# Splitting the merged tiles earlier, a longer own tail in the output projection, and weight units split one step sooner in the recurrent layer

## The reference

```python
# first model, each layer
merged = (gates[:, :, 0] * (y_a @ w_pa[l])
          + gates[:, :, 1] * (y_b @ w_pb[l])
          + gates[:, :, 2] * (y_c @ w_pc[l]))
x = x + merged @ w_o[l]
h = rms_norm(x, g_ffn[l])
x = x + (jax.nn.silu(h @ w1[l]) * (h @ w3[l])) @ w2[l]

# second model, recurrent layer (6 blocks of 256 channels)
proj = x @ w_in
y_branch, u = jnp.split(proj, 2, axis=-1)
y_branch = jax.nn.gelu(y_branch, approximate=True)
u = conv4(u) + conv_b
r, i = sigmoid(gates(u))
log_a = -LRU_C * r * jax.nn.softplus(-a_param)
a = jnp.exp(log_a)
b = jnp.sqrt(-jnp.expm1(2.0 * log_a)) * (i * u)
h = scan(a, b)              # h[t] = a[t] * h[t-1] + b[t]
return (h * y_branch) @ w_out

# second model, behind each mixer and each network
x = x + rms_norm_2(m, norm_g[layer, 1])
```

## Time and profile before

| what | value |
|---|---|
| median of 3 runs | 3479.68 us (3471.39, 3479.68, 3499.27) |
| profiled execution | 3500.03 us, its span 3498.2 us |
| TensorE busy | 3414.9 us, 98% of the span |
| VectorE / ScalarE / GpSimd busy | 45% / 34% / 10% |
| mean granted TensorE clock | 0.982 of full speed |

### The profile page before, as it was taken

The page is one execution under the profiler, slowest core; times in us unless marked ns, Lnnn a source line. Parts: engine busy times, 40 slices in busy tenths (PEclk is TensorE's granted clock), DMA queues, the critical chain, the costliest instruction groups (busy, mean ns, idle before and its releaser), DMA issues.

```text
span 3498.2 us, 41531 instructions
## 1 busy us (share of the span) xinstructions
PE 3414.9 (98%) x17076; PEld 2817.6 (81%) x17076; DVE 1576.8 (45%) x2298; ACT 1186.5 (34%) x1931; POOL 339.0 (10%) x309
## 2 busy tenths in 40 slices
PE   8999999999999999999999999999999998999998
PEld 7777887788887867887888888888888887788887
DVE  5454444443445452444433443343533357764234
ACT  4334322322324242323322332222422236643222
POOL 2120000100020110000000110001200031130001
PEclk9999999999999997999999999999999999999999
DMA  4120222222231211222222222222232222222222
GB/s 150 61 73 30 69 98 91 90 97 97 92 104 61 81 40 35 73 97 85 92 98 99 93 98 76 88 82 73 79 102 97 97 73 73 91 85 94 93 97 78
DMA packets 83242, 295.47 MB, mean 84 GB/s; under 512 B 9616, under 2 KB 11888, under 8 KB 82928
## 3 DMA queue, kind: packets, MB, share of 16 engines
q1 hardware_dynamic: 80352, 283.85, 24.1%
q0 software_dynamic: 2704, 8.98, 0.8%
HBM read 289.61 MB, written 3.18 MB: 84 GB/s over the span
## 4 chain that ended last, share of the span: by engine, by line
PE 89%; DVE 5%; ACT 4%; issue 1%; POOL 1%; DMA 0%; SPq 0%; DVEq 0%; ACTq 0%; POOLq 0%
PE bank L2289 26%; PE bank L2291 25%; PE bank L2290 25%; PE bank L2534 3%; PE bank L2502 3%; PE bank L2511 2%; DVE w_lo L1745 1%; PE bank L2648 1%; ACT w_hi L1340 1%; DVE arena L2199 1%; PE bank L2442 1%; ACT arena L1519 1%; PE bank L2358 1%; PE bank L2636 0%; ACT arena L1378 0%
## 5 line engine op out<-in xcount | busy, mean ns | idle before, releaser
L1745 DVE TENSOR_TENSOR w_lo<-raw_ring,w_hi 128x1024 fp32r<-128x1024 f32 x530 | 674.7, 1274 | 1302.6 <-ACT w_hi L1340 1301.7
L2289 PE MATMUL bank<-h_hi,w_hi 128*128 128x512 f32 (+1 forms) x2752 | 1075.9, 391 | 42.9 <-DVE w_lo L1745 19.1
L2290 PE MATMUL bank<-h_lo,w_hi 128*128 128x512 f32 (+1 forms) x2752 | 1060.7, 385 | 0.0
L2291 PE MATMUL bank<-h_hi,w_lo 128*128 128x512 f32 (+1 forms) x2752 | 1060.4, 385 | 0.0
L1340 ACT ACTIVATE w_hi<-raw_ring 128x1024 fp32r<-128x1024 f32 x530 | 559.9, 1057 | 1154.2 <-PE bank L2291 1079.1
L2289 PEld LDWEIGHTS bank<-h_hi,w_hi 128*128 128x128 f32 x2752 | 524.2, 190 | 155.2 <-issue 32.4
L2290 PEld LDWEIGHTS bank<-h_lo,w_hi 128*128 128x128 f32 x2752 | 524.2, 190 | 102.5 <-issue 3.1
L2291 PEld LDWEIGHTS bank<-h_hi,w_lo 128*128 128x128 f32 x2752 | 523.5, 190 | 103.3
L2289 PE MATMUL bank<-act_hi,w_hi 128*128 128x512 f32 (+1 forms) x1336 | 508.7, 381 | 10.6 <-DVE act_lo L1758 7.6
L2291 PE MATMUL bank<-act_hi,w_lo 128*128 128x512 f32 (+1 forms) x1336 | 505.4, 378 | 0.0
L2290 PE MATMUL bank<-act_lo,w_hi 128*128 128x512 f32 (+1 forms) x1336 | 505.3, 378 | 0.0
(11 more groups left out here) (195 smaller groups left out, 2720.4 us busy)
## 6 DMA issues: line engine op xcount, KB each, us to landing
raw_ring<-weights SPq DMA_DIRECT2D x530, 512.0 KB, 3.3
arena<-rpb POOLq DMA_DIRECT2D x16, 320.0 KB, 4.3
xs<-x_t SPq DMA_DIRECT2D x8, 256.0 KB, 6.5
out_t<-xs SPq DMA_DIRECT2D x16, 128.0 KB, 1.8
arena<-block SPq DMA_DIRECT2D x1, 1024.0 KB, 9.6
arena<-o_nat POOLq DMA_DIRECT2D x2, 512.0 KB, 3.4
arena<-ret POOLq DMA_DIRECT2D x4, 256.0 KB, 3.1
o_nat<-arena POOLq DMA_DIRECT2D x2, 384.0 KB, 3.1
```

The lines of the kernel that those rows point to most:

```text
L1745: nc.vector.tensor_tensor(w_slot(w_lo, u), raw_slot(u), f32(w_slot(w_hi, u)), ALU.subtract) \
L2289: nc.tensor.matmul(out, lhs[0], rhs[0], start=first, stop=False)
L2290: nc.tensor.matmul(out, lhs[0], rhs[1], start=False, stop=False)
L2291: return nc.tensor.matmul(out, lhs[1], rhs[0], start=False, stop=last)
```

## The change

Four edits; no arithmetic is added or taken away.

1. `MERGED_EARLY = 6`: ScalarE and VectorE split merged tiles 0 to 5 between `("pr", 7, 1)` and the last gate, and only tiles 6 and 7 after `("pr", 7, 2)`.
2. `WO_TAIL = 4`: in the output projection the last four k tiles run group by group.
3. Recurrent layer: ScalarE splits one unit between the two high parts of the convolution and no longer between the two gelu; VectorE splits one more unit between the two scans of a block, and none between the two row products.
4. `post_norm`: the squares of X tiles 0 to 3 move behind the high parts of tiles 4 to 7, those of 4 to 7 behind everything; ScalarE splits a unit after the high part of tile 5, VectorE splits it between the low parts of tiles 6 and 7 and no longer ahead of both.

```diff
+WO_TAIL = 4
+MERGED_EARLY = 6
...
-    together = n - 2 if keys[0][1] == "wo" else n
+    together = n - WO_TAIL if keys[0][1] == "wo" else n
...
                     following_hi(1, k)
+                    if k == 5:
+                        upto(first[-1], 2, 1)
+                    if k >= NT:
+                        square(X[k - NT], tile(SQ2 + k - NT), D ** -0.5)
+                upto(first[-1], 5, 1)
+                for k in range(NT, KD):
                     square(X[k], tile(SQ2 + k), D ** -0.5)
-                    if k in (5, 7):
-                        upto(first[-1], 2 if k == 5 else 5, 1)
...
+                        if (m, b) == (KD - 1, 2):
+                            before((l, "pr", KD - 1, 1))
+                            wait_acc(act, (l, "pr", KD - 1, 1))
+                            merged_hi(l, range(MERGED_EARLY))
                         copy_out((l, "gate", m, b), tile(GATE + 3 * (m % 2) + b), func=ACT.Sigmoid)
...
                 before((l, "pr", KD - 1, 2))
                 wait_acc(act, (l, "pr", KD - 1, 2))
-                for m in range(KD):
-                    act.wait_ge(merged_ready, KD * l + m + 1)
-                    hi(("merged", l, m), part(act_hi, m), tile(MERGED + m))
+                merged_hi(l, range(MERGED_EARLY, KD))
...
-                    def conv_hi(n):
+                    def conv_hi(n, between=None):
                         for i in (2 * n, 2 * n + 1):
+                            if between and i % 2:
+                                before(between)
                             act.wait_ge(conv_ready, i + 1)
...
-                            conv_hi(n + 1)
+                            conv_hi(n + 1, ("ly", 2 * n + 3) if n else None)
...
-                    if j in (2 * KD - 1, 2 * KD + 1):
-                        upto(first[-1], 2 if j < 2 * KD else 5, 1)
+                    if j >= 2 * KD:
+                        upto(first[-1], 2 if j == 2 * KD else 5, 1)
...
                     if kind == "gate":
+                        if (m, i) == (KD - 1, 2):
+                            merged_lo(l, range(MERGED_EARLY))
                         rows_scaled((l, "gate", m, i))
...
-                            conv(n + 1, [("lg", n, 1, 0), ("ly", 2 * n + 2) if n else ("lu", 4)])
+                            conv(n + 1, [("ly", 2 * n + 2), ("ly", 2 * n + 3)] if n else [("lg", 0, 1, 0), ("lu", 4)])
...
                         for i in pair:
-                            before(after)
+                            before(("lg", n + 1, 0, 0) if i % 2 and n < LRU_BLOCKS - 2 else after)
```

More of the change, by code:

```diff
@@ L1561, in first_inputs, with merged_hi @@
                     square(X[k], tile(SQ1 + k), D ** -0.5)
+            def merged_hi(l, ms):
+                for m in ms:
+                    act.wait_ge(merged_ready, KD * l + m + 1)
+                    hi(("merged", l, m), part(act_hi, m), tile(MERGED + m))
             for l in range(DEPTH):
@@ L2043, in ffn, with merged_lo @@
                         lo_x(*following[:2], KD - 1, following[2])
+            def merged_lo(l, ms):
+                for m in ms:
+                    lo(("merged", l, m), part(act_lo, m), tile(MERGED + m), part(act_hi, m))
             dve.wait_ge(consts_in, 16)
@@ L2123, in _ @@
                         then(ins)
-                for m in range(KD):
-                    lo(("merged", l, m), part(act_lo, m), tile(MERGED + m), part(act_hi, m))
+                merged_lo(l, range(MERGED_EARLY, KD))
                 for m in range(KD):
```

## The result

| what | before | after |
|---|---|---|
| median | 3480.95 us (17 runs, 3466.68 to 3502.69) | 3450.96 us (17 runs, 3441.54 to 3473.41) |
| profiled execution | 3500.03 us | 3471.89 us, its span 3470.1 us |
| mean granted TensorE clock in it | 0.982 | 0.985 |

The ratio is 0.9906, its 95% interval 0.9881 to 0.993: 0.9% faster. The forecast was 3452.3 us, and 3472.6 us for a profiled execution with the long stretch at half clock.

What follows compares the result with a forecast made beforehand. TensorE, busy 98% of the span, bounds the kernel; only its waits and half-clock time can be won back. -21.4 (projections) - 6.9 (recurrent layer) + 0.9 (norms) = -27.4 us, from 3479.7 to 3452.3; range 3437 to 3475.

Steps and rivals of the forecast that it cites:

- the long stretch at half clock: First model, from the second attention group: 28.9 us lost in the profiled execution's layer 1; rival puts it in median, chance 0.28.
- the forecast case: Whole kernel: median 3452.3 us, own range 3444 to 3461, chance 0.45.
- No wait: End of the output projection: VectorE keeps up, so TensorE does not wait for the last tiles.
- The next product wants tile 7 only at its last k tile: Behind the output projection: tile 7 is wanted only 4.8 us into the next product.
- the sum of 3.4 us: Behind the projection's last group: unit 1.23, addition 0.68, high part 0.73, low part 0.75, plus handover.
- two signs of being right: Both projection stretches: 54 to 55 us for 240 matmuls, and no wait on the low parts of X.
- the 21.4 of the sum: Projection stretches of both layers: edits 1 and 2 win back all lost time, 9.4 and 12.0 us.
- The lap of 31.71: Recurrent layer: time from square roots to square roots before the change, forecast to become 30.0 us.
- The new waits ahead of lg: Recurrent layer: TensorE waits for lg(n+1)'s unit about 2.8 us a block, around 5 in the first.
- the ring opens: Rival, recurrent layer: it becomes TensorE's, 20.7 us won there, -41.2 in all, 3438.5 us; chance 0.09.
- the bound of -6: Second model's norms: uncontended operations take 0.48 + 1.23 + 0.48, both waits vanish, 2.0 us a norm won.
- Nothing in the edits speaks for or against: Rival that the half-clock stretch falls into the median run: edits give no reason either way, 3472.6 us; chance 0.28.

Runs made afterwards that it cites:

- z_after_wait: Changed kernel, with VectorE's four low parts made ahead of its two weight units in layer 1's attention: 3442.55 us.
- y_wait: Kernel before, with only VectorE's four low parts made ahead of its two weight units in layer 1's attention: median 3466.28 us.
- x_norm2: Changed kernel, with ScalarE's squares of tiles 0 to 3 behind all high parts in the three norms, so GpSimd adds later: 3436.8 us.
- e3_ring: Kernel before with the third edit alone, the recurrent layer: 3471.53 us, ratio 0.9998.
- e4_norms: Kernel before with the fourth edit alone, the three norms of the second model: 3476.76 us, ratio 0.9992.
- e1_merged: Kernel before with the first edit alone, six merged tiles split while the last gate's product runs: 3458.97 us, ratio 0.9944.
- e2_wo: Kernel before with the second edit alone, the output projection's last four k tiles group by group: 3457.59 us, ratio 0.9940.

## Why the prediction was right

**The time.** 3450.96 against 3452.3: right, and by the forecast case. A part of it is luck, since two errors cancel. The forecast started from 3479.7, the middle one of three runs; in the 17 runs of the comparison those without the long stretch have a median of 3472.9, and those of the changed kernel one of 3449.6, 23.3 less. Between z_after_wait and y_wait it is 23.7, not 27.4. The rest of the 30.0 us between the medians comes from the long stretch, which fell into fewer runs: 2 of 17 against 7 of 17 of before. The forecast left it where it was.

**Edit 1: right, step by step.** Six high parts took 3.24 us (forecast 3.2), six low parts 3.70 (3.7), the last gate was taken up at 584.20 (584.6), and no wait followed. Together with edit 2 the clock stayed at 1.00 in both stretches, as forecast.

**Edit 2: right in size, wrong in "No wait".** The step that failed is "The next product wants tile 7 only at its last k tile". It looked at tile 7 alone. In the program the low part of tile 6 stands behind the addition of tile 7, and that behind the unit; TensorE wants tile 6 one k tile sooner. Nor did the sum of 3.4 us hold VectorE's idle time for w_hi, 1.60, and the longer w_lo, 2.00 for 1.23. What remained was 0.96 us a layer, 1.40 with the handover (55.80 less 54.40), so two signs of being right did not come: 54 to 55 us, and no wait on the low parts of X. The other error went the other way: the stretch before takes 66.3 to 66.4 us in layer 0 too in three other executions of the same code, not 63.8. Together: 2 x (66.37 - 55.80) = 21.1, against the 21.4 of the sum: two errors of 2 to 3 us that cancel. In the two profiled executions it was 18.6 (8.0 and 10.6).

**Edit 3: right.** From the roots of block 0 to those of block 4 are 119.00 us, where before (2912.89 to 3038.68) there were 125.79: 6.79 less, forecast 6.9. (The lap of 31.71 that the forecast took is the longest of four from 31.03, and the new ones are 29.40, 29.62, 30.36 and 29.62, not 30.0; in the sum this cancels.) The new waits ahead of lg were forecast at 5 in the first block and 2.8 behind it; they are 5.13, 0.55 and 2.90. The 0.55 stands behind a piece at half clock of 3.4 us, in which TensorE's own work took 1.7 us longer: the wait was filled, and the lap stayed nearly the ring's (29.62, with 30.36 for the next). The rival "the ring opens" is refuted: even with the lap cut to 28.96 the wait stays.

**Edit 4: right.** Forecast +0.3 a norm, with a wait of some 2 us ahead of tile 7. The wait is 2.32. Between the same waits, in pairs of traces with as much half-clock time, the three stretches behind the norms are longer by 0.3 us each (379.8 against 379.5, 50.1 against 49.8, 370.1 against 369.8): +1.0 against +0.9. With GpSimd's additions moved behind them the three operations were in time (x_norm2), so the reason for rejecting the bound of -6 was right.

**The long stretch: right in size, wrong in "Nothing in the edits speaks for or against".** The profiled execution had it and took 3471.89 (forecast with it 3472.6); the median had not. The wait behind which it begins, 1.75 us, was in the trace already, and the prediction does not name it. Among the kernels that keep that wait, those without edits 1 and 2 (before, e3_ring, e4_norms) have it in 45 of 115 runs, those with either (after, e1_merged, e2_wo and the kernels built on after) in 9 of 71. The edits seem to make it rarer, though they leave the wait as it is; so the wait's length alone does not decide. Why the same wait opens it in some runs and never in layer 0 is open.

**What stays open.** The pieces read from traces add to 21.1 + 7.4 - 1.0 = 27.5 us (the recurrent layer, from its first wait to the norm behind it: 211.1 to 211.8 us in five traces with the edit, 217.7 to 219.4 in five without), the medians of z_after_wait and y_wait to 23.7. The 3.8 us between them are of the size of the pieces at half clock that differ from run to run, and of the 3.6 us by which the kernel before differs between the two comparisons; no run pins them down.

## What to carry to other kernels

Read what a lost stretch costs from more than one execution before subtracting it, and follow each wait on to what the clock did behind it. A wait of 1.75 us, too small to be worth an edit by its own length, went with a loss of 30 us in two runs of five, and the loss went with the wait. Before moving a weight unit, write down for the consumer each tile that stands behind it, not only the last one. And where VectorE and GpSimd overlap, moving GpSimd's trigger by 1.5 us can do what another order of VectorE's own work did not: it took away the wait that edit 4 had only moved.

## What was unexpected of the hardware

A wait of 1.75 us was followed by 61.4 us at half clock, and in another execution by 13.7. In the same execution the waits of 2.98 and 3.19 us in either layer were followed by at most 6.8 us at half clock. In the 61.4 us TensorE was busy without a gap of note: the row 1289.40:1350.80 shows 61.40 us busy of 61.40.

The clock also falls without a wait. In x_norm2, behind the second norm, 18.8 us without a wait of 0.1 us at clock 1.00 (the wait of 0.97 us ends just before them) are followed by 6.8 us at half clock, TensorE busy throughout:

```profile
2811.10:2817.90 6.80, 6.80 (x23) 5.92 (x24) 0.32 (x1) 0.26 (x1) 1.04 (x1) 0.50 0.25 80
2792.30:2811.10 18.80, 18.75 (x135) 17.59 (x135) 13.14 (x20) 11.96 (x20) 13.80 (x12) 1.00 0.26 85
```
